# The last projection of a two-block transformer kernel: three of its sixteen pairs of units in seven products instead of two, and the sums of the activations that they need made one to two units sooner

## The reference

```
mixed = jnp.concatenate([o_a * silu(sb_gate), o_b * silu(mla_gate)], axis=-1)   # 256 x 2048
y = mixed @ w_out                                                               # w_out: 2048 x 2048
return x + rms_norm(y, post_norm_w)
```

## Time and profile before

| | us |
|---|---|
| median of 3 runs | 1251.65 (1250.95 to 1251.79) |
| the profiled execution | 1251.29 |
| its span, first to last instruction | 1249.2 |
| PE busy | 1239.6 (99%) |
| DVE busy | 929.0 (74%) |
| ACT busy | 805.0 (64%) |
| mean granted clock of TensorE | 0.999 of full speed |

### The profile page before, as it was taken

The page is one execution under the profiler, slowest core; times in us unless marked ns, Lnnn a source line. Parts: engine busy times, 40 slices in busy tenths (PEclk is TensorE's granted clock), DMA queues, the critical chain, the costliest instruction groups (busy, mean ns, idle before and its releaser), DMA issues.

```text
span 1249.2 us, 16239 instructions
## 1 busy us (share of the span) xinstructions
PE 1239.6 (99%) x5879; PEld 1032.6 (83%) x5879; DVE 929.0 (74%) x1471; ACT 805.0 (64%) x1257; POOL 204.8 (16%) x149
## 2 busy tenths in 40 slices
PE   9999999999999999999999999999999999999998
PEld 7888888888888888888788888889988888888886
DVE  5497898477787677898877775767678788576686
ACT  5798798765657556565666675447755555666653
POOL 1499999910000000000000010000000000000000
PEclk9999999999999999999999999999999999999999
DMA  9899998944566666667555556566765556655564
GB/s 348 273 256 247 270 254 244 268 165 144 179 200 186 188 184 185 205 187 216 156 164 153 164 156 188 183 189 166 195 175 168 168 153 197 192 167 154 185 199 137
DMA packets 133566, 243.86 MB, mean 195 GB/s; under 512 B 12144, under 2 KB 22512, under 8 KB 133360
## 3 DMA queue, kind: packets, MB, share of 16 engines
q1 hardware_dynamic: 129600, 229.40, 59.4%
q0 software_dynamic: 3600, 13.11, 5.3%
q10 hardware_dynamic: 288, 0.32, 0.1%
HBM read 227.60 MB, written 2.10 MB: 184 GB/s over the span
## 4 chain that ended last, share of the span: by engine, by line
PE 93%; DVE 3%; DMA 1%; ACT 1%; issue 0%; DVEq 0%; SPq 0%; ACTq 0%
PE PS L2059 27%; PE PS L2061 26%; PE PS L2060 26%; PE PS L1969 2%; PE PS L2101 2%; PE PS L2103 2%; PE PS L2102 2%; PE PS L1988 2%; DMA w_raw<-in_w_kv 1%; DVE w_lo L1243 1%; PE PS L2271 1%; PE PS L2167 0%; DVE aux L1262 0%; PE PS L2169 0%; PE PS L2168 0%
## 5 line engine op out<-in xcount | busy, mean ns | idle before, releaser
L717 ACT ACTIVATE w_hi<-w_raw 128x1024 fp32r<-128x1024 f32 (+2 forms) x383 | 393.3, 1029 | 314.7 <-PE PS L2061 263.0
L1243 DVE TENSOR_TENSOR w_lo<-w_raw,w_hi 128x1024 fp32r<-128x1024 f32 (+2 forms) x339 | 400.1, 1183 | 207.2 <-ACT w_hi L717 206.3
L2059 PE MATMUL PS<-w_hi,actA_hi 128*128 128x512 f32 x720 | 282.3, 392 | 0.0
L2061 PE MATMUL PS<-w_hi,actA_lo 128*128 128x512 f32 x720 | 280.6, 390 | 0.0
L2060 PE MATMUL PS<-w_lo,actA_hi 128*128 128x512 f32 x720 | 280.3, 389 | 0.0
L2059 PE MATMUL PS<-w_hi,actB_hi 128*128 128x512 f32 (+1 forms) x618 | 244.2, 395 | 0.0
L2061 PE MATMUL PS<-w_hi,actB_lo 128*128 128x512 f32 (+1 forms) x618 | 238.7, 386 | 0.0
L2060 PE MATMUL PS<-w_lo,actB_hi 128*128 128x512 f32 (+1 forms) x618 | 238.1, 385 | 0.0
L2061 PEld LDWEIGHTS PS<-w_hi,actA_lo 128*128 128x128 f32 x720 | 135.2, 188 | 28.9
L2059 PEld LDWEIGHTS PS<-w_hi,actA_hi 128*128 128x128 f32 x720 | 135.1, 188 | 27.6
L2060 PEld LDWEIGHTS PS<-w_lo,actA_hi 128*128 128x128 f32 x720 | 135.2, 188 | 27.4
(11 more groups left out here) (419 smaller groups left out, 1609.2 us busy)
## 6 DMA issues: line engine op xcount, KB each, us to landing
w_raw<-in_a_w_in SPq DMA_DIRECT2D x95, 512.0 KB, 5.9
w_raw<-in_w_in SPq DMA_DIRECT2D x88, 512.0 KB, 3.8
w_raw<-in_w_kv SPq DMA_DIRECT2D x64, 512.0 KB, 3.8
w_raw<-in_b_w_in SPq DMA_DIRECT2D x64, 512.0 KB, 3.8
w_raw<-in_a_w_out SPq DMA_DIRECT2D x32, 512.0 KB, 3.8
w_raw<-in_b_w_out SPq DMA_DIRECT2D x32, 512.0 KB, 3.7
w_raw<-in_w_out SPq DMA_DIRECT2D x32, 512.0 KB, 4.2
tap_products<-tap_products POOLq DMA_DIRECT2D x25, 512.0 KB, 8.2
```

Of the source, the lines that this page charges most:

```text
L717: nc.scalar.activation(split_slot(u)[0][:, f:2 * w], w_raw[:, RAW_SLOT[u], f:2 * w], ACT.Copy)\
L1243: V.tensor_tensor(wl, w_raw[:, RAW_SLOT[u], f:2 * w], wh.bitcast(F32), ALU.subtract)\
L2059: T.matmul(bank, ah, wh[:, kk, :], start=(first or opens_last and tok == 1) and kk == 0, stop=False)
L2061: ins = T.matmul(bank, al, wh[:, kk, :], start=False, stop=last and kk == 1)
```

## The change

The table `SEVEN` says which pairs of a group are done in seven products, and `OUT_ACTS_AT` at which turns the sums of the activations are made.

```
-         dict(c=C_OUT2 + 1, which="A", quads=(3, 5), kept=2)]
+         dict(c=C_OUT2 + 1, which="A", quads=(2, 4, 6), kept=2)]
...
-OUT_ACTS_AT = [FIRST[C_OUT2] + at for at in (7, 8, 9, 11)]
+OUT_ACTS_AT = [FIRST[C_OUT2] + at for at in (6, 7, 8, 9)]
...
-                if u == OUT_ACTS_AT[3] - 1:
+                if u == OUT_ACTS_AT[2]:
                     act.wait_ge(S["out_acts"], 1)
                     chunk_done(act, C_OUT2 - 1)
                     nc.scalar.activation(out_sums(flat_b(hi)), out_sums(aux[:, 4 * H8:5 * H8]), ACT.Copy)\
```

## The result

The changed kernel takes 1253.95 us (median of 13 runs, 1252.87 to 1255.90) against 1251.45 for the kernel before beside it (13 runs, 1250.75 to 1252.08). The ratio is 1.0022 with a 95% interval of 1.0015 to 1.0030, so it is 2.5 us slower. Predicted were 1254.4 us and 0.22% slower. The interval lies wholly above 1, so the loss is clear of the noise, but 0.2%, the line for which the prediction gave its chances, lies inside it.

A forecast was written before the change was run, and what follows sets the result against it. The prediction took PE as the bound, busy 1239.6 of 1249.2 us. It summed -0.68 + 1.9 + 1.5 = +2.7 us onto 1251.29, giving 1254.0, plus 0.36 for the median: 1254.4 us, range 1253.0 to 1255.6.

The forecast's parts named there:

- the line for which the prediction gave its chances: Whole kernel: a 0.2% difference; chances slower 0.60, within 0.2% 0.38, faster 0.02.
- The gain: Last projection: one more pair in seven products saves 3 matmuls on PE, -0.68 us.
- the other pairs: U16 and U20: pairs start 10.20 us apart, so no further wait, 0 us each.
- the end of the group: U24, chunk 58, needs chunk 56 finished: 0.3 us in time, taken as 0, with 0.4 allowed.
- The first deadline: U10, first unit of chunk 57: late squares delay y_scaled for the banks of chunk 55; PE waits 1.9 us.
- the longer steps 0 and 1: DVE ahead of the split for U10: some 0.5 and 0.25 us more, fitting into idle time, so nothing taken.
- The restart: PE at U10 and U12: the old pace resumes 0.22 us behind the release by DVE.
- The second deadline: U12: differences ahead of DVE's split make PE wait another 1.5 us; U12 starts 3.4 us late in all.
- the bank's wait: U10: PE's wait for the banks of chunk 55 to be scaled, 1.9 us.
- The allowance for late loads: U16: the weights of U17 may land late and delay the split; taken as 0, with 0.3 us allowed.
- The clock: Rival: the granted clock falls after PE's waits at U10 and U12; 1257 us or more, chance 0.03.
- Its price for a fall: Behind the waits: a 12-matmul unit at the lower clock takes 5.44 us instead of 2.72; one gives 1257.1.

The follow-up runs named there:

- squares_first: Changed kernel with ACT's squares of chunk 55 moved ahead of its rounding of the sums at turn U8; 1253.07 us, ratio 1.0018 to the kernel before.
- one_rounding_more: Changed kernel plus one unused 128x1024 ACT instruction right ahead of the rounding of the sums; 1255.72 us, ratio 1.0039 to the kernel before.
- spread: Changed kernel with sums made at U5, U6, U7, rests at U9, and ACT's rounding at U9; 1251.26 us, ratio 1.0002 to the kernel before.
- spread_split_first: As spread, with DVE's split for U12 ahead of the first pair's differences and two slots' loads waiting for them; 1251.51 us, ratio 1.0004.
- old_turns: Kernel before with three pairs in seven products, the sums left at their old turns; 1257.95 us, ratio 1.0053 to the kernel before.

## Why the prediction was right

**The gain** of 0.68 us: the lost 3.32 less 0.68 is 2.64, and the stretch measured 2.69. The 0.05 between them is all that the other pairs and the end of the group cost.

**The first deadline**: forecast 1.9 us lost at U10, measured 1.85. Each term can be checked against a row: L1375 and L1376 0.55 and 0.56 (0.56), L971 1.49 (1.47), 1.40 from its start to the squares (1.40), 1.24 for the squares from 1181.99 to 1183.23 (1.24). That the longer steps 0 and 1 would fit into DVE's idle time held too: ahead of the split for U10 the idle time shrank from 0.43 to 0.22 us, and the split started on time. The restart took 0.16 us behind L2419's end at 1184.05, where I had taken 0.22.

**The second deadline**: forecast 3.4 us in all, measured 3.32. The experiments show more than the agreement: without the bank's wait 2.17 us remain (squares_first), and ACT's time passes on one to one (one_rounding_more). So the two waits are one chain, as the prediction had it, and mending the first alone did not bring the gain. No kernel here brought it whole: the best two with three pairs, spread and spread_split_first, are as fast as the kernel before.

**The other pairs**: 0 us, measured 10.20 apart. The allowance for late loads was too narrow: the loads cost 0.37 us in spread and 0.3 in spread_split_first, where I had allowed 0.3 for U16 alone and nothing for U20.

**The end of the group**: no wait at U24, as forecast, with DVE's additions for chunk 56 done at 1221.19 and U24's first matmul at 1221.76, about 0.3 us in time with the restart.

**The size of the whole**: the forecast gave +2.7 and the stretch shows +2.69; the medians give +2.5. The forecast lay 0.45 us over the measured median; of that, 0.2 is the median of before, which came out lower in the longer series. So near a hit in the median is partly luck, as the timed executions of the changed kernel lie up to 3.0 us apart for a reason that is not known; what the experiments bear out is the stretch. The clock, to which the prediction gave 0.03, stayed at 1.00 through both waits in all three profiled executions. Here are the windows of the first:

```profile
1180.00:1185.00 5.00, 3.42 (x16) 2.50 (x15) 2.64 (x4) 4.41 (x7) 0.00 (x0) 1.00 0.38 132
1185.00:1190.00 5.00, 4.88 (x22) 3.67 (x20) 4.86 (x6) 1.39 (x3) 0.00 (x0) 1.00 0.35 105
```

The prediction had only the rows of the end of the kernel to go by, and they are a weak guide. Its price for a fall, 2.72 us for 12 matmuls, was a little high: they cost 2.4 more in old_turns.

## What to carry to other kernels

Where the busiest engine never waits, write down its starts as a grid of deadlines, and check a change of the order against each deadline that it brings forward: here three matmuls saved were worth 0.68 us and two deadlines moved by one and two units cost 3.32. A helper step put ahead of a step that frees a buffer delays the buffer by the helper's own wait as well as its work, and shares of busy time (DVE 75%) don't show it. Time such a change by a stretch inside the profile when the effect is near what the whole time can resolve, and take more than one execution: the stretches agree to 0.15 us, while in one_rounding_more the median moved by 1.15 us more than the stretch.

## What the runs showed of the hardware

The clock. PE idle for 1.6, 1.9 and 2.5 us (changed, squares_first, one_rounding_more) left the granted clock at 1.00; idle for 4.59 us it fell to 0.50 before PE resumed, and the next 12 matmuls started 0.43 us apart. Behind a wait that cost 4.9 us came so another 2.4 us, half as much again. But the length of a gap alone does not tell when the clock falls. Behind the last matmul (L2385) PE is idle to the end in every execution, and the clock fell 0.3 us behind that matmul's recorded end in the third execution of squares_first, 0.9 and 1.4 in its other two, 2.3 in that of before and 2.9 in the first of the changed kernel. These are the last matmul and the window in which the clock fell, for the two that lie furthest apart of these (columns as above):

```profile
1245.74 1.10 PE L2385 MATMUL PS<-aux,work 128*128 128x512 f32 x2 [1.50 <-DVE work L1943]
1247.00:1248.00 1.00, 0.00 (x0) 0.00 (x0) 0.57 (x1) 0.47 (x1) 0.00 (x0) 0.58 0.68 250
...
1246.04 1.10 PE L2385 MATMUL PS<-aux,work 128*128 128x512 f32 x2 [1.50 <-DVE work L1943]
1250.00:1251.00 1.00, 0.00 (x0) 0.00 (x0) 0.00 (x0) 0.00 (x0) 0.00 (x0) 0.54 0.19 70
```

So that the waits of up to 2.5 us in the middle left the clock alone is what these executions show, and no proof that they always do.

PE's restart. It took up its full pace 0.16 us behind the end of DVE's scaling at U10 and 0.22 behind DVE's split at U12, and its slower pace 0.50 us behind L1379 in old_turns.
